# Routing of a PEER layer: second choice's one-hots in float16, scores used up in place, slots turned and first low parts made inside the first quarter of U

## The chip, the cores and the metric

The kernel runs on one core of a Trainium2 chip. The metric is the device time of one execution in microseconds (us); of several runs the median is given. A profiled execution has a time of its own, which is used for sums made from its rows. Engines: PE is TensorE, DVE is VectorE, ACT is ScalarE, POOL is GpSimd, SP is SyncE (it issues the weight transfers).

## The reference, cut to what matters

The model is a two-layer decoder step for 256 prompt tokens and 32 sample tokens, 288 tokens in all. Layer 0 is a gated MLP mixer, layer 1 dilated attention; each is followed by a PEER block, in which every token chooses 16 of 16384 experts in each of 8 heads:

```
q = (h @ w_q).reshape(T, PEER_HEADS, 2, D_HALF)
s = einsum('thpe,pke->thpk', q, sub_keys)                 # 2 x 128 scores a head
s1, i1 = top_k(s[:, :, 0], 16);  s2, i2 = top_k(s[:, :, 1], 16)
cand = s1[..., :, None] + s2[..., None, :]                # 256 candidates
top_s, top_c = top_k(cand, 16)
e1 = take_along_axis(i1, top_c // 16);  e2 = take_along_axis(i2, top_c % 16)
g = softmax(top_s)
a = einsum('td,thkd->thk', h, u_tab[e1 * 128 + e2])
coef = g * gelu(a)
out = einsum('thk,thkd->td', coef, v_tab[e1 * 128 + e2])
```

## The kernel before

Instead of gathering experts it multiplies all tokens by all of U (gelu of the result is C, laid out expert by token), scales C by a dense matrix of gates that is zero but at the chosen experts, and multiplies by all of V. The 128 tiles of 128 experts are taken in four quarters of 32 (`EQ`). `up` is a quarter of U, `down` one of V; the order is U0, U1, V0, U2, V1, U3, V2, V3 in each layer. U0 is done in plain float32 (`up_whole`: 32 tiles of 8 matmuls, PSUM banks 0 to 3 in turn). All other quarters split both operands into a high part (ScalarE, `upper_part`, for half a weight block) and a low part (VectorE, `lower_part`) and make three faster matmuls of each (`product`, L690, L691, L696).

Routing is done by VectorE during U0. `route(m, src, heads)` treats one tile of tokens: first the sample tile (m = 2, 2 heads' worth in 128 rows), then in a loop the two prompt tiles (m = 0, 1; 8 heads). `top16` finds the 16 largest scores with their places, two rounds of 8, and overwrites what it has found; for the prompt tiles a copy S of the scores S2 is made first (L1517), because a loop register picks the tile. The candidates are summed (L1495), `top16` again, then the two numbers of each choice are looked up: the place in the candidates is split into two (L1504, L1505), each is compared with 0..15 (L1508, 16 one-hots for 16 choices in 8 heads: 2048 elements), multiplied by the indices of the first selection (L1511) and reduced (L1514), all in float32. The results go to `eg`.

When the third tile is routed, VectorE raises `exp_in`; ScalarE takes the exponential (L1166); VectorE sums it, takes the reciprocal and scales (L1529 to L1534) and raises `slot_ready`. TensorE then transposes `eg` (`slot_transposes`, L644 and L648), VectorE copies the turned slots out of PSUM (L1552) and makes float16 copies (L1555 to L1559). From these come, during U1, the one-hots by token groups (`one_hot_group`, L1570 to L1579), whose product on TensorE is the gates (`gate_groups`, L664), applied by `apply_gates` (L1589). C's high and low parts are made at the start of a `down` (L1104, L1599).

Everything is ordered by hand: each engine has its own list, and semaphores count banks filled and emptied (`act_full`, `act_free`, `dve_full`, `dve_free`), blocks begun by TensorE (`blocks_begun`, on which SP reloads the ring of four 1 MB blocks), and high and low parts made (`hi_made`, `lo_made`). On TensorE `slot_transposes()` stands behind the whole of U0; on ScalarE the exponential and the first three high parts stand behind the activations of U0 (L1162); U1 on TensorE waits until the slots have been copied (`dve_free` at `D0["V"]`), for `h_lo` and for its first low part.

Of the kernel before, what the change touches and what calls it, by code (L numbers as in the profile page):

```python
# [32 lines left out]
ALU = mybir.AluOpType  # L33
# [64 lines left out]

GATE_LAG = 7
# [50 lines left out]
def build(nc, i, o):  # L150
    A0, D0 = starts(TO_ACT), starts(TO_DVE)
    with ExitStack() as ctx:
# [37 lines left out]
        iota_top, _ = place("iota_top", [P, TOP])  # L190
# [45 lines left out]
        S = view(big, EQ * T, HP, NK)  # L236
        cand = view(big, EQ * T + 2048, PH, TOP * TOP)
        eq = view(big, EQ * T + 4096, PH * TOP, TOP)
        tv = view(work, 0, HP, TOP)
        ti = work[:, 256:512].bitcast(U32).rearrange("p (a b) -> p a b", a=HP)  # L240
        tif = view(work, 512, PH, 2, TOP)
# [3 lines left out]
        posf = view(work, 1280, 2, PH * TOP)  # L245
# [197 lines left out]
        def _(pe):  # L443
# [177 lines left out]
            def peer(layer):  # L621
# [46 lines left out]
                def up_whole(q):  # L668
# [4 lines left out]
                    with pe.Fori(0, 2) as it:  # L673
                        for bl in range(8):
                            r = arrived(n0 + bl, it, 2)
                            for j in range(2 * bl, 2 * bl + 2):
                                pe.wait_ge(act_free, it * 16 + (k0 + j - 3))
                                for c in range(DC):
                                    at = ((j % 2) * DC + c) * P
                                    last = pe.matmul(ps[:, j % 4, 0:T], ring[:, r, at:at + P], hT[:, c, :],  # L680
                                                     start=(c == 0), stop=(c == DC - 1))
                                    if c == 0 and j % 2 == 0:
                                        last.then_inc(blocks_begun, 1)
                                last.then_inc(act_full, 1)
# [56 lines left out]
                slot_transposes()  # L741
# [245 lines left out]
        def _(act):  # L987
# [80 lines left out]
            def peer(layer):  # L1068
# [90 lines left out]
                with act.Fori(0, EQ // 8) as it:  # L1159
                    for j in range(8):  # L1160
                        act.wait_ge(act_full, it * 8 + (k0 + j + 1))
                        act.activation(C[:, 0, it * 8 + j, :], ps[:, j % 4, 0:T],  # L1162
                                       ACT.Gelu_apprx_tanh).then_inc(act_free, 1)

                act.wait_ge(exp_in, layer + 1)
                act.activation(gs, gs, ACT.Exp).then_inc(exp_out, 1)  # L1166
                for k in range(HI_LEAD):
                    upper_part(k)
# [104 lines left out]
        def _(dve):  # L1273
# [16 lines left out]

            def loop(n, per, body):

                n0 = count["n"]
                with dve.Fori(0, n) as it:
                    count["it"], count["per"] = it, per
                    body(it)
# [516 lines left out]
```

## Time and profile before

| | |
|---|---|
| median of 3 runs | 2414.11 us (2413.97 to 2414.7) |
| profiled execution | 2412.68 us, span 2410.9 us |
| PE busy | 2327.2 us, 97% of the span |
| DVE busy | 1590.8 us, 66% |
| ACT busy | 852.1 us, 35% |
| DMA | 348.93 MB, mean 145 GB/s |

The page gives busy times over the span, the chain of work that ended last, the costliest groups of instructions, and the DMA issues. Spans of matmuls overlap, so their mean duration is more than the time from one to the next. The profile can also be asked for the instructions in order of time, and for the busy time and the granted clock of TensorE in a stretch.

### The profile page before, as it was taken

Reading aid. Unit: us, or ns where it says so; the run is one execution under the profiler, and the core shown is the slowest. Engines: PE = TensorE matmul, PEld = TensorE weight load, DVE = VectorE, ACT = ScalarE, POOL = GpSimd, SP = SyncE. Lnnn points to the kernel's source line nnn. Section 1 sums busy time; section 2 is a strip of 40 time slices with the busy share of each in tenths; the row PEclk is TensorE's granted clock in tenths of the full one; section 3 lists DMA queues with packets and bytes.
Section 4 is the critical chain, followed back from the end, with each engine's and each line's share of the span. In section 5 each row is a group of like instructions: output and inputs, shape, how many; then the busy total and the mean of one; then the engine's idle time right before and its main releaser. Section 6 shows DMA issues by size and latency. Waiting matters only on the chain.

```text
span 2410.9 us, 47698 instructions
## 1 busy us (share of the span) xinstructions
PE 2327.2 (97%) x19577; PEld 2171.9 (90%) x19577; DVE 1590.8 (66%) x3496; ACT 852.1 (35%) x1137; POOL 55.8 (2%) x95
## 2 busy tenths in 40 slices
PE   7999999999999999999999999989999999999996
PEld 5889877999999999998987797789899999999996
DVE  5566599778755864686423359987787378548743
ACT  4534212342253244324323232133424432542432
POOL 1000000000000000002031000000000000000000
PEclk9999999999999999999999999999999999999998
DMA  5434343433454444446473243434344444444341
GB/s 205 162 105 158 123 140 110 142 133 127 140 171 157 140 141 173 141 141 215 162 245 129 87 139 123 139 122 141 123 140 150 164 141 139 163 169 141 124 155 72
DMA packets 51507, 348.93 MB, mean 145 GB/s; under 512 B 6369, under 2 KB 6385, under 8 KB 11665
## 3 DMA queue, kind: packets, MB, share of 16 engines
q1 hardware_dynamic: 44928, 324.16, 39.4%
q0 software_dynamic: 6448, 22.96, 3.0%
q8 instruction: 91, 1.49, 0.3%
q14 instruction: 40, 0.32, 0.0%
HBM read 342.83 MB, written 4.26 MB: 144 GB/s over the span
## 4 chain that ended last, share of the span: by engine, by line
PE 93%; ACT 3%; DVE 3%; issue 1%; DMA 0%; POOL 0%; DVEq 0%; ACTq 0%; POOLq 0%
PE ps L690 21%; PE ps L696 19%; PE ps L691 19%; PE ps L680 10%; PE ps L664 5%; PE ps L904 1%; PE ps L537 1%; ACT C_hi L1104 1%; PE ps L538 1%; PE ps L539 1%; PE ps L826 1%; PE ps L802 1%; PE ps L578 1%; PE ps L580 1%; PE ps L582 1%
## 5 line engine op out<-in xcount | busy, mean ns | idle before, releaser
L1544 DVE TENSOR_TENSOR w_lo<-ring,w_hi 128x1024 fp32r<-128x1024 f32 x448 | 544.0, 1221 | 268.0 <-ACT w_hi L1094 261.3
L1094 ACT ACTIVATE w_hi<-ring 128x1024 fp32r<-128x1024 f32 x448 | 473.3, 1058 | 638.0 <-PE ps L691 637.0
L690 PE MATMUL ps<-C_hi,w_hi 128*128 128x288 f32 x2048 | 627.3, 306 | 20.9 <-DVE C_lo L1599 20.6
L696 PE MATMUL ps<-C_hi,w_lo 128*128 128x288 f32 x2048 | 606.8, 296 | 0.0
L691 PE MATMUL ps<-C_lo,w_hi 128*128 128x288 f32 x2048 | 606.5, 296 | 0.0
L690 PE MATMUL ps<-h_hi,w_hi 128*128 128x288 f32 x1536 | 461.6, 301 | 4.1 <-DVE slots L1552 4.1
L691 PE MATMUL ps<-h_lo,w_hi 128*128 128x288 f32 x1536 | 454.9, 296 | 0.0
L696 PE MATMUL ps<-h_hi,w_lo 128*128 128x288 f32 x1536 | 453.3, 295 | 0.0
L690 PEld LDWEIGHTS ps<-C_hi,w_hi 128*128 128x128 f32 x2048 | 387.5, 189 | 26.5 <-DVE C_lo L1599 19.4
L691 PEld LDWEIGHTS ps<-C_lo,w_hi 128*128 128x128 f32 x2048 | 388.5, 190 | 0.0
L696 PEld LDWEIGHTS ps<-C_hi,w_lo 128*128 128x128 f32 x2048 | 387.9, 189 | 0.0
L690 PEld LDWEIGHTS ps<-h_hi,w_hi 128*128 128x128 f32 x1536 | 289.3, 188 | 4.3 <-issue 4.3
L696 PEld LDWEIGHTS ps<-h_hi,w_lo 128*128 128x128 f32 x1536 | 290.7, 189 | 0.0
L691 PEld LDWEIGHTS ps<-h_lo,w_hi 128*128 128x128 f32 x1536 | 290.0, 189 | 0.0
L680 PE MATMUL ps<-hT,ring 128*128 128x288 f32 x1024 | 248.8, 406 | 2.2 <-ACT mid L1155 2.2
L680 PEld LDWEIGHTS ps<-hT,ring 128*128 128x128 f32 x1024 | 194.4, 190 | 56.3 <-ACT mid L1155 2.7
L1116 ACT ACTIVATE big<-ps 128x288 f32 (+1 forms) x192 | 79.1, 412 | 351.5 <-PE ps L696 351.5
L1574 DVE TENSOR_TENSOR hots<-iota_twice,halves 128x1024 f16<-128x1024 f16 x288 | 196.7, 683 | 0.0
L664 PE MATMUL ps<-hots 128*128 128x32 f16 x4608 | 163.6, 177 | 0.0
L1606 DVE TENSOR_TENSOR xT<-xT,ps 128x288 f32<-128x288 f32 x64 | 29.1, 454 | 193.7 <-PE ps L696 193.7
L664 PEld LDWEIGHTS ps<-hots 128*128 128x128 f16 x4608 | 135.0, 97 | 21.1
L1579 DVE TENSOR_TENSOR hots<-hots,parts 128x256 f16<-128x256 f16 x576 | 139.7, 283 | 0.0
(252 smaller groups left out, 2508.9 us busy)
## 6 DMA issues: line engine op xcount, KB each, us to landing
ring<-in_U SPq DMA_DIRECT2D x128, 1024.0 KB, 4.9
ring<-in_V SPq DMA_DIRECT2D x128, 1024.0 KB, 4.9
ring<-in_peer_q SPq DMA_DIRECT2D x16, 1024.0 KB, 4.9
ring<-in_w_in_v SPq DMA_DIRECT2D x8, 1024.0 KB, 6.1
ring<-in_w_in_u SPq DMA_DIRECT2D x8, 1024.0 KB, 4.9
ring<-in_w_out SPq DMA_DIRECT2D x8, 1024.0 KB, 4.9
big<-in_cache POOLq DMA_DIRECT2D x16, 512.0 KB, 6.3
big<-in_cache POOLq DMA_DIRECT2D x48, 128.0 KB, 6.5
```

The source lines that it names most:

```text
L537: one = pe.matmul(out, ew_hi[:, h % HI_SLOTS, at], eh_hi[:, c, :], start=(c == 0), stop=False)
L664: g = pe.matmul(ps[:, 6 + j % 2, t * EQ:(t + 1) * EQ], hot1[:, j % RH, t // 2, :, t % 2], hot2[:, j % RH, c, t // 2, :, t % 2], start=(c = ...
L680: last = pe.matmul(ps[:, j % 4, 0:T], ring[:, r, at:at + P], hT[:, c, :], start=(c == 0), stop=(c == DC - 1))
L690: one = pe.matmul(out, w_hi[:, h % HI_SLOTS, at], hi, start=start, stop=False)
L691: two = pe.matmul(out, w_hi[:, h % HI_SLOTS, at], lo, start=False, stop=False)
L696: return pe.matmul(out, w_lo[:, h % (2 * R), at], hi, start=False, stop=stop)
L1094: act.activation(w_hi[:, k % HI_SLOTS, :], ring[:, bl % R, (k % 2) * HBLK:(k % 2 + 1) * HBLK], ACT.Copy).then_inc(hi_made, 1)
L1116: act.activation(C[:, q % 2, e, :], ps[:, h % 4, 0:T], ACT.Gelu_apprx_tanh).then_inc(act_free, 1)
L1544: dve.tensor_tensor(w_lo[:, n % (2 * R), :], ring[:, n // 2 % R, n % 2 * HBLK:(n % 2 + 1) * HBLK], w_hi[:, n % HI_SLOTS, :], ALU.subtract) ...
L1574: dve.tensor_tensor(hot1[:, s], iota_twice[:].unsqueeze(1).broadcast_to((P, pairs, NK, 2)), halves[:, 0, tok].rearrange("p (a t) -> p a t" ...
L1579: last = dve.tensor_tensor(hot2[:, s, c], here2, parts[:, c, tok].rearrange("p (a t) -> p a t", t=2).unsqueeze(2) .broadcast_to((P, pairs, ...
L1606: dve.tensor_tensor(xT[:, dc, :], xT[:, dc, :], ps[:, 4 + dc % 2, 0:T], ALU.add).then_inc(dve_free, 1)
```

## The change

The second lookup (the numbers of each choice) is done in float16: one-hots with the 16 places as the outermost dimension, elements in pairs, the sum over the places as four additions of halves in place of a reduction. The operands are copied as float16 beforehand (`tif` with each element twice, `posf` reordered). The prompt tiles are routed straight from S2, which is used up, without the copy and without the loop. The transposes of the slots stand ahead of tile 30 of U0 on TensorE (`SLOTS_EARLY = 2`); the exponential on ScalarE stands ahead of the activation of tile 28, and the first three high parts ahead of those of tiles 29, 30 and 31. The loops of `up_whole`, of its activations and of the routing are written out. `iota_top` goes; `iota_twice`, which the gates use already, takes its place.

```diff
--- before.py
+++ after.py
@@ -96,6 +96,8 @@
 HI_LEAD, LO_LEAD = 3, 2
 SPLIT = 7 * EQ
 
+SLOTS_EARLY = 2
+
 GATE_LAG = 7
 
 CCHUNKS = [(0, 1), (1, 3), (3, 6), (6, 10), (10, 14), (14, 19), (19, 25), (25, 32)]
@@ -187,7 +189,6 @@
         halves, _ = place("halves", [P, 2, T], F16)
         parts, _ = place("parts", [P, GATE_PARTS, T], F16)
         iota_twice, _ = place("iota_twice", [P, NK, 2], F16)
-        iota_top, _ = place("iota_top", [P, TOP])
         ident, _ = place("ident", [P, P])
         tmask, _ = place("tmask", [P, NS])
         ones, _ = place("ones", [P, P])
@@ -233,16 +234,16 @@
         qT = view(wide, 0, HP, T)
         S2 = view(mid, 0, 2, HP * NK)
         Ssam = view(mid, 2 * HP * NK, 2 * SH, NK)
-        S = view(big, EQ * T, HP, NK)
         cand = view(big, EQ * T + 2048, PH, TOP * TOP)
-        eq = view(big, EQ * T + 4096, PH * TOP, TOP)
+
+        eq = big[:, EQ * T + 4096:EQ * T + 5120].bitcast(F16)
         tv = view(work, 0, HP, TOP)
         ti = work[:, 256:512].bitcast(U32).rearrange("p (a b) -> p a b", a=HP)
-        tif = view(work, 512, PH, 2, TOP)
+        tif = work[:, 512:768].bitcast(F16).rearrange("p (s c) -> p s c", s=2)
         cs = view(work, 768, PH, TOP)
         pos = work[:, 896:1024].bitcast(U32)
         pos12 = work[:, 1024:1280].bitcast(U32).rearrange("p (a b) -> p a b", a=2)
-        posf = view(work, 1280, 2, PH * TOP)
+        posf = work[:, 1280:1408].bitcast(F16).rearrange("p (s n) -> p s n", s=2)
         gs = view(work, 1536, 2 * PH + SH, TOP)
         gsum = view(work, 1920, 2 * PH + SH)
         grec = view(work, 1944, 2 * PH + SH)
@@ -670,18 +671,18 @@
                     n0 = state["block"]
                     k0 = A0[f"U{layer}"] + q * EQ
                     pe.wait_ge(act_free, A0[f"U{layer}"])
-                    with pe.Fori(0, 2) as it:
-                        for bl in range(8):
-                            r = arrived(n0 + bl, it, 2)
-                            for j in range(2 * bl, 2 * bl + 2):
-                                pe.wait_ge(act_free, it * 16 + (k0 + j - 3))
-                                for c in range(DC):
-                                    at = ((j % 2) * DC + c) * P
-                                    last = pe.matmul(ps[:, j % 4, 0:T], ring[:, r, at:at + P], hT[:, c, :],
-                                                     start=(c == 0), stop=(c == DC - 1))
-                                    if c == 0 and j % 2 == 0:
-                                        last.then_inc(blocks_begun, 1)
-                                last.then_inc(act_full, 1)
+                    for j in range(EQ):
+                        r = arrived(n0 + j // 2)
+                        if j == EQ - SLOTS_EARLY:
+                            slot_transposes()
+                        pe.wait_ge(act_free, k0 + j - 3)
+                        for c in range(DC):
+                            at = ((j % 2) * DC + c) * P
+                            last = pe.matmul(ps[:, j % 4, 0:T], ring[:, r, at:at + P], hT[:, c, :],
+                                             start=(c == 0), stop=(c == DC - 1))
+                            if c == 0 and j % 2 == 0:
+                                last.then_inc(blocks_begun, 1)
+                        last.then_inc(act_full, 1)
                     state["block"] += EQ // 2
 
                 def product(out, h, tile, hi, lo, start, stop):
@@ -738,7 +739,6 @@
 
                 pe.wait_ge(h_ready, (1 + 2 * layer) * DC + DC)
                 up_whole(0)
-                slot_transposes()
                 pe.wait_ge(dve_free, D0[f"V{layer}"])
                 pe.wait_ge(h_lo_made, layer + 1)
                 up(1, 0)
@@ -1156,16 +1156,15 @@
                 act.wait_ge(h_ready, (1 + 2 * layer) * DC + DC)
                 act.activation(h_hi[:], hT[:], ACT.Copy).then_inc(h_hi_made, 1)
                 k0 = A0[f"U{layer}"]
-                with act.Fori(0, EQ // 8) as it:
-                    for j in range(8):
-                        act.wait_ge(act_full, it * 8 + (k0 + j + 1))
-                        act.activation(C[:, 0, it * 8 + j, :], ps[:, j % 4, 0:T],
-                                       ACT.Gelu_apprx_tanh).then_inc(act_free, 1)
-
-                act.wait_ge(exp_in, layer + 1)
-                act.activation(gs, gs, ACT.Exp).then_inc(exp_out, 1)
-                for k in range(HI_LEAD):
-                    upper_part(k)
+                for j in range(EQ):
+                    if j == EQ - SLOTS_EARLY - 2:
+                        act.wait_ge(exp_in, layer + 1)
+                        act.activation(gs, gs, ACT.Exp).then_inc(exp_out, 1)
+                    if j >= EQ - SLOTS_EARLY - 1 and j - (EQ - SLOTS_EARLY - 1) < HI_LEAD:
+
+                        upper_part(j - (EQ - SLOTS_EARLY - 1))
+                    act.wait_ge(act_full, k0 + j + 1)
+                    act.activation(C[:, 0, j, :], ps[:, j % 4, 0:T], ACT.Gelu_apprx_tanh).then_inc(act_free, 1)
                 up(0, 1)
                 down(1, split=0)
                 up(2, 2, split=1)
@@ -1287,15 +1286,6 @@
 
                 step(ins)
                 last_step()
-
-            def loop(n, per, body):
-
-                n0 = count["n"]
-                with dve.Fori(0, n) as it:
-                    count["it"], count["per"] = it, per
-                    body(it)
-                assert count["n"] == n0 + per, (count["n"] - n0, per)
-                count["it"], count["n"] = None, n0 + n * per
 
             def full(stage, k):
                 dve.wait_ge(dve_full, D0[stage] + k + 1)
@@ -1400,7 +1390,6 @@
 
             link(dve.tensor_reduce(tmask[:], ident[:].rearrange("p (a s) -> p s a", s=NS), AXX, ALU.add))
             dve.tensor_scalar(tmask[:], tmask[:], -1.0, 1.0e30, ALU.add, ALU.mult)
-            dve.tensor_copy(iota_top[:], iota[:, 0:TOP])
             dve.tensor_copy(iota_twice[:], iota.unsqueeze(2).broadcast_to((P, NK, 2)))
             dve.wait_ge(mix_loaded, 16 * 7)
             dve.tensor_tensor(wsp, wsp, maskp.unsqueeze(1).broadcast_to((P, AG, P)), ALU.mult)
@@ -1496,33 +1485,47 @@
                                            tv4[:, :, 0, :].unsqueeze(3).broadcast_to((P, heads, TOP, TOP)),
                                            tv4[:, :, 1, :].unsqueeze(2).broadcast_to((P, heads, TOP, TOP)), ALU.add))
                     link(top16(cs, pos.rearrange("p (a b) -> p a b", a=PH), cand, heads))
-                    dve.tensor_tensor(gs[:, bass.ds(m * PH, heads), :], cs[:, 0:heads, :],
+                    dve.tensor_tensor(gs[:, m * PH:m * PH + heads, :], cs[:, 0:heads, :],
                                       cs[:, 0:heads, 0:1].broadcast_to((P, heads, TOP)), ALU.subtract)
 
-                    dve.tensor_copy(tif.rearrange("p h s k -> p (h s k)")[:, 0:2 * n],
-                                    ti.rearrange("p a b -> p (a b)")[:, 0:2 * n])
                     dve.tensor_scalar(pos12[:, 0, 0:n], pos[:, 0:n], 4, None, ALU.logical_shift_right)
                     link(dve.tensor_scalar(pos12[:, 1, 0:n], pos[:, 0:n], 15, None, ALU.bitwise_and))
-                    link(dve.tensor_copy(posf[:, :, 0:n], pos12[:, :, 0:n]))
+                    half = TOP // 2
                     for s in range(2):
-                        link(dve.tensor_tensor(eq[:, 0:n, :], posf[:, s, 0:n].unsqueeze(2).broadcast_to((P, n, TOP)),
-                                               iota_top[:].unsqueeze(1).broadcast_to((P, n, TOP)), ALU.is_equal))
-                        eq4 = eq.rearrange("p (h k) j -> p h k j", h=PH)[:, 0:heads]
-                        link(dve.tensor_tensor(eq4, eq4,
-                                               tif[:, 0:heads, s, :].unsqueeze(2).broadcast_to((P, heads, TOP, TOP)),
-                                               ALU.mult))
-                        link(dve.tensor_reduce(eg[:, bass.ds(m, 1), s, 0:n], eq[:, 0:n, :], AXX, ALU.add))
-
-                def route_prompt(m):
-                    link(dve.tensor_copy(S.rearrange("p a b -> p (a b)").unsqueeze(1), S2[:, bass.ds(m, 1), :]))
-                    route(m, S, PH)
+                        dve.tensor_copy(
+                            tif[:, s, 0:2 * n].rearrange("p (j h t) -> p j h t", j=TOP, h=heads),
+                            ti.rearrange("p (h s) k -> p s k h", s=2)[:, s, :, 0:heads].unsqueeze(3).broadcast_to(
+                                (P, TOP, heads, 2)))
+                        last = dve.tensor_copy(
+                            posf[:, s, 0:n].rearrange("p (k h t) -> p k h t", k=half, h=heads),
+                            pos12[:, s, 0:n].rearrange("p (h k t) -> p k h t", h=heads, k=half))
+                    link(last)
+                    for s in range(2):
+                        link(dve.tensor_tensor(
+                            eq[:, 0:TOP * n].rearrange("p (j c t) -> p j c t", j=TOP, t=2),
+                            posf[:, s, 0:n].rearrange("p (c t) -> p c t", t=2).unsqueeze(1).broadcast_to((P, TOP, n // 2, 2)),
+                            iota_twice[:, 0:TOP, :].unsqueeze(2).broadcast_to((P, TOP, n // 2, 2)), ALU.is_equal))
+                        eq3 = eq[:, 0:TOP * n].rearrange("p (j k c) -> p j k c", j=TOP, k=half)
+                        link(dve.tensor_tensor(
+                            eq3, eq3,
+                            tif[:, s, 0:2 * n].rearrange("p (j c) -> p j c", j=TOP).unsqueeze(2).broadcast_to(
+                                (P, TOP, half, 2 * heads)), ALU.mult))
+
+                        for k in (8, 4, 2):
+                            link(dve.tensor_tensor(eq[:, 0:k * n], eq[:, 0:k * n], eq[:, k * n:2 * k * n], ALU.add))
+                        link(dve.tensor_tensor(
+                            eg[:, m, s, 0:n].rearrange("p (h k t) -> p k h t", h=heads, k=half),
+                            eq[:, 0:n].rearrange("p (k h t) -> p k h t", k=half, h=heads),
+                            eq[:, n:2 * n].rearrange("p (k h t) -> p k h t", k=half, h=heads), ALU.add))
 
                 dve.wait_ge(act_free, A0[f"U{layer}"])
                 route(2, Ssam, SH)
                 dve.wait_ge(h_hi_made, layer + 1)
                 dve.tensor_tensor(h_lo[:], hT[:], h_hi[:], ALU.subtract).then_inc(h_lo_made, 1)
-                loop(2, 1 + 3 + 1 + 1 + 3 + 1 + 2 + 6, route_prompt)
-                dve.wait_ge(dstep, count["n"])
+                for m in range(2):
+
+                    route(m, S2[:, m, :].rearrange("p (a k) -> p a k", a=HP), PH)
+                last_step()
 
                 dve.engine_nop().then_inc(exp_in, 1)
                 dve.wait_ge(exp_out, layer + 1)
```

## Rows read from the trace of the kernel before

**Rows 1.** Page: the chain that ended last, by engine.
```profile
PE 93%; ACT 3%; DVE 3%; issue 1%; DMA 0%; POOL 0%; DVEq 0%; ACTq 0%; POOLq 0%
```

**Rows 2.** By stretch: length, busy us (count) of PE, PEld, DVE, ACT, POOL; PEclk, DMA, GB/s.
```profile
278.00:402.50 124.50, 124.40 (x512) 97.20 (x512) 120.77 (x493) 19.55 (x36) 0.00 (x0) 1.00 0.39 135
402.50:410.20 7.70, 2.09 (x32) 1.61 (x31) 6.10 (x13) 7.21 (x8) 0.00 (x0) 0.74 0.00 0
410.20:530.00 119.80, 119.80 (x1331) 117.17 (x1332) 97.08 (x219) 43.22 (x62) 0.00 (x0) 0.99 0.41 141
```

**Rows 3.** Chain in order of time, layer 0: start, us, what.
```profile
278.10 124.44 PE ps L680 x512
...
403.09 1.28 ACT L1166
404.39 0.45 ACT work L1166
...
408.73 1.11 DVE slots L1552 x3
...
410.15 0.60 PE ps L690
```

**Rows 4.** The same chain, layer 1.
```profile
1450.93 124.44 PE ps L680 x512
...
1582.98 0.60 PE ps L690
```

**Rows 5.** Stretches behind the hole, columns as in rows 2.
```profile
410.10:413.20 3.10, 3.05 (x13) 3.05 (x14) 2.96 (x10) 0.00 (x0) 0.00 (x0) 0.53 0.36 71
1583.00:1587.30 4.30, 4.30 (x18) 4.30 (x19) 4.16 (x13) 2.34 (x2) 0.00 (x0) 0.51 0.57 198
```

**Rows 6.** VectorE in order of time: start, us, operation [idle before].
```profile
333.96 0.29 DVE L1499 TENSOR_TENSOR work<-work 128x128 f32 x1 [0.52 <-DVE work L1486]
...
349.80 1.23 DVE L1517 COPY big<-mid 128x2048 f32 x1 [0.56 <-DVE work L1514]
351.07 0.29 DVE L1472 MAX8 work<-big 128x8 f32<-128x128 f32 x1
...
388.11 0.29 DVE L1499 TENSOR_TENSOR work<-work 128x128 f32 x1 [0.29 <-DVE work L1486]
388.32 0.28 DVE L1502 CAST work<-work 128x256 f32<-128x256 uint32 x1
...
389.24 2.29 DVE L1508 TENSOR_TENSOR big<-work,iota_top 128x2048 f32<-128x2048 f32 x1
...
401.11 2.29 DVE L1514 TENSOR_REDUCE work<-big 128x2048 f32 x1
```

**Rows 7.** Groups of VectorE instructions by shape: busy us, mean ns.
```profile
L1574 DVE TENSOR_TENSOR hots<-iota_twice,halves 128x1024 f16<-128x1024 f16 x25 | 17.1, 685 | 0.0
L1579 DVE TENSOR_TENSOR hots<-hots,parts 128x256 f16<-128x256 f16 x50 | 12.2, 284 | 0.0
...
L1511 DVE TENSOR_TENSOR big<-big,work 128x2048 f32<-128x2048 f32 x4 | 9.2, 2292 | 0.1
...
L1511 DVE TENSOR_TENSOR big<-big,work 128x512 f32<-128x512 f32 x2 | 1.4, 691 | 0.1
```

**Rows 8.** TensorE in order of time at the transposes.
```profile
406.51 1.54 PE L644 MATMUL ps<-ident,work 128*128 128x128 f32 x6 [3.98 <-DVE work L1534]
...
1579.33 0.87 PE L644 MATMUL ps<-ident,work 128*128 128x128 f32 x6 [3.98 <-DVE work L1534]
...
1580.13 0.39 PE L648 MATMUL ps<-ident,work 32*32 32x32 f32 x24
```

**Rows 9.** ScalarE in order of time, end of the first quarter.
```profile
394.90 0.41 ACT L1162 ACTIVATE big<-ps 128x288 f32 x1 [3.47 <-PE ps L680]
```

**Rows 10.** Page: DMA issues, last number us to landing.
```profile
ring<-in_U SPq DMA_DIRECT2D x128, 1024.0 KB, 4.9
```

**Rows 11.** An unrolled stretch of TensorE, columns as in rows 2.
```profile
225.00:245.00 20.00, 19.98 (x150) 19.77 (x149) 16.10 (x24) 6.73 (x7) 0.00 (x0) 1.00 0.51 172
```

## The prediction, as put on record before the change was run

> **What bounds the kernel now.** I read the chain of waits by engine first [rows 1]: TensorE carries 93% of it, so a change pays only where it removes time in which TensorE stands still or runs slowly, or where it delays TensorE. Next the busy time by stretch round the changed place [rows 2]. In the first quarter of U (278 to 402.5) TensorE is busy 124.40 of 124.50 us, in the 7.7 us behind it 2.09 us, and in the quarter after that 119.80 of 119.80. VectorE is the one that is late: it is busy 120.77 us in the first stretch and its routing isn't done when TensorE is. The chain in order of time [rows 3] shows what fills the hole: TensorE's 512 matmuls end at 278.10 + 124.44 = 402.54, the exponential runs at 404.39, the turned slots are copied at 408.73, and the next quarter starts at 410.15. Layer 1 has the same chain [rows 4]: 1450.93 + 124.44 = 1575.37, next start 1582.98. Hole: 7.61 us in each layer, of which the slot transposes themselves are a part. Last, the clock behind the hole [rows 5]: granted 0.53 over 410.10 to 413.20 and 0.51 over 1583.00 to 1587.30, that is, nearly all at the lower level (1.2 GHz), after 4 us without any matmul and then only a few transposes.
>
> **The change, part by part.**
>
> *Two prompt tiles of routing on VectorE.* They use scores in place, so the copy goes: from its start 349.80 to the next instruction 351.07 is 1.27 us, twice, 2.5 us [rows 6]. The loop over them goes too: 0.56 us idle at its turn, and 0.52 us (first pass, and 0.29 in the second) ahead of L1499, the instruction addressed by a register, 1.4 us in all [rows 6].
>
> From L1499 to the end of the last reduction it is 388.11 to 403.40, 15.29 us a tile [rows 6]: 1.13 us of preparation, then six float32 passes over 2048 elements. The two float32 casts in it become four float16 ones; a 256-element cast takes 0.28 us, and it starts 0.08 us before the end of the independent instruction ahead of it [rows 6], so two of them are some 0.5 of the 1.13, 0.6 stay, and the new four take about 1.0 us, and 1.6 if the strided and repeated reads go at one element per cycle. Preparation 1.6 us, high end 2.2. The one-hots: float16 two-input instructions take 685 ns for 1024 elements and 284 ns for 256, so 0.15 us + 0.522 ns an element; float32 ones take 2292 ns for 2048 and 691 ns for 512, so 0.16 us + 1.042 ns [rows 7]. Per choice: compare and multiply, 2048 each, 2 x 1.22; sums in halves of 1024, 512 and 256, 0.69 + 0.42 + 0.28; the last of 128 into float32 taken at the float32 rate, 0.29. That is 4.12 us, and six waits on the result at 0.04 each (the copy at 349.80 takes 1.23 and its reader starts at 351.07), 4.36. Two choices: 8.7 us. Tail 10.3 against 15.29: 5.0 saved a tile, 10.0 for both. The sample tile (512 elements, six float32 passes of 0.69) goes from about 5.1 to 4.8 with the same two formulas: 0.2. Total 2.5 + 1.4 + 10.0 + 0.2 = 14.1 us, so the routing ends at 403.40 - 14.1 = 389.3.
>
> The compare and the multiply read operands that are repeated along an outer dimension and contiguous only in pairs (or in 16s). The row of L1574 has just that form of compare at 0.52 ns an element, and L1579 that of the multiply. The Trainium skill (VectorE: DVE Perf Modes, the section on how modes are chosen) says that a two-input instruction doubles its rate only if every tensor is 16-bit with step 1; this would leave the last sum, which writes float32, at the single rate. No row has such a mixed sum. By that page the sum is as above; at the double rate it would be 0.3 us shorter in all, hidden either way.
>
> *What the earlier end releases.* From the end of routing to the first transpose it is now 403.40 to 406.51 = 3.1 us, with a table load of 1.28 at 403.09 in front of the exponential [rows 3, 8, 9]. In the new order ScalarE comes to the exponential behind tile 27's activation (28 tiles, 278.10 + 28 x 3.889 = 387.0, plus 0.5), so the load runs 387.5 to 388.8, ahead of the scores. Exponential 389.4 to 389.8, the 1.67 us of reduction, reciprocal and scaling as before (404.84 to 406.51): slots ready at 391.5. TensorE arrives at the transposes ahead of tile 30, at 278.10 + 30 x 3.889 = 394.8. Slack 3.3 us: no wait.
>
> *The transposes.* They are not removed, only moved: 6 large and 24 small, 1579.33 to about 1580.52 = 1.2 us in layer 1 [rows 8]. In the new place they are between matmuls, so all 1.2 us are paid. U ends at 403.7.
>
> *ScalarE's moved work.* The activation of tile 28 has the second table load before it: exponential out 389.8, load to 391.1, tile full at 390.9; 0.2 us late, and its bank is wanted only by the next quarter's first tile. The three high parts (1.06 each) go in front of the activations of tiles 29, 30, 31, where ScalarE now idles 3.47 of each 3.88 us [rows 9]. Their blocks are in the ring: SP's reload waits for blocks that TensorE has begun, in the same order as before; the block for the third part is issued when tile 28 begins (387.0) and a block lands in 4.9 us [rows 10]. SP's queue itself isn't changed, and POOL's isn't passed.
>
> *VectorE behind the slots.* First low part 392.9 to 394.1, second 396.3 to 397.5 (it waits for the second high part), three copies 1.2, halves and parts 1.5, two groups of one-hots 2.6: done about 403. TensorE's next quarter wants the slots copied, one low part and a free bank at 403.7: all there. VectorE then waits for tile 31's activation (404.2) before its third low part, which TensorE wants two rounds of some 3.3 us later. So nothing is late next, and the hole closes entirely. If the float16 casts or sums cost up to 3.3 us more than worked out, still nothing; beyond it each microsecond is a stall of one in each layer.
>
> *Unrolled code.* TensorE's, ScalarE's and VectorE's loops are now written out. TensorE's unrolled projection of 225 to 245 runs 150 matmuls in 20.00 us, 0.133 each with nothing lost [rows 11], faster issue than the 0.243 needed here. And the loop's 512 matmuls are at 0.243 throughout, so its turn costs nothing now. Taken: 0, bounds -0.3 and +1.5 us a layer. The Trainium skill (Runtime: NRT & Kernel Launch, Instruction fetch mechanics) says that a taken branch can force a fetch stall and straight code is prefetched; by it the unrolling might also give TensorE something at the turn, but the constant 0.243 shows nothing to give, and on VectorE the 0.56 is in the sum already.
>
> *Clock.* TensorE never idles before the quarter, so I expect the 0.51 to 0.53 rows to become 1.00. 13 matmuls in 3.10 us would take 13 x 0.133 = 1.73: 1.4 saved; 18 in 4.30 would take 2.4: 1.9 saved [rows 5, 11].
>
> **The sum.** Per layer 7.61 - 1.2 = 6.4; twice 12.8; clock 1.4 + 1.9 = 3.3; together 16.1 us. The profiled execution took 2412.68 us (span 2410.9): 2396.6. The median of the runs is 2414.11, 1.43 above it, so in terms of the median **2398.0 us**.
>
> **Rivals.**
> *A, the slots come late by a little.* The four casts, the strided last sum or the extra dependent waits cost more than 3.3 us above my 14.1. For it: none of these forms has a row, and there are six dependent steps a choice where there were three. Against it: even all sums at one element per cycle add 4 x 0.95 = 3.8 and the casts 1.2, 5.0 together, 1.7 over the slack. 2 x 1.7 = 3.4 back, and perhaps no loss of clock for so short a stop: 2401.4.
> *B, the float16 passes run at the single rate.* Then a choice costs 2 x 2.29 + 1.22 + 0.69 + 0.43 + 0.29 + 0.24 = 7.45 us, two tiles 29.8 for the one-hots instead of 17.4; with the slower casts (1.2 more) routing ends at 389.3 + 12.4 + 1.2 = 402.9 and the slots are ready at 405.1 or later. TensorE stands at tile 30 from 394.8, 10.3 us instead of 6.4 net, because the two tiles that used to cover the wait now lie behind it; the clock drops there as it did before. 3.9 lost a layer: 2414.1 + 7.8 = 2421.9. It decides against the change once the slots are ready after 394.8 + 6.4 = 401.2. Against: L1574 and L1579 [rows 7].
> *C, given back downstream.* The next quarter would be bound by VectorE and eat the gain. For it: VectorE is busy 97.08 of 119.80 us there [rows 2], and C_lo later makes TensorE wait. Against: 23 us idle, TensorE busy all 119.80, and VectorE's own start there moves forward by about 10 us, more than TensorE's. If half of the gain went: 2406.
> *D, nothing gained*, something unseen on the path in place of the hole (fetching code, a reload): 2414.
>
> **How the numbers follow.** Forecast 0.83 (2395 to 2400.5), A 0.06, B 0.03, C 0.04, D 0.04. Changes under 0.2%, 4.8 us, can't be told from none here. Forecast, A and C are faster; D is no change or slightly slower; B slower: 0.93, 0.03, 0.04. The range reaches from 2394.5 (unrolling gains, routing's end lets VectorE run ahead and shortens a later C_lo wait) to 2403, which takes in A.
>
> **What would show it.** The row of the quarter's 512 matmuls grows from 124.4 to some 125.7 from first start to the next quarter's first, with the transposes inside it and no wait on the slots. The last routing instruction ends near 389.3 (wrong if after 392.6). L1508's successor, the float16 compare of 2048, takes 1.2 us, not 2.3. The 0.51 and 0.53 clock rows are 1.00. The next quarter and the C_lo waits keep their length. I am wrong if TensorE shows a wait at the transposes, if any 3 us of it are at half clock behind U's first quarter, or if the C_lo waits grow by microseconds.

## The result and the profile after

| | before | after |
|---|---|---|
| median, first comparison | 2414.4 us (2413.97 to 2416.77) | 2394.74 us (2394.41 to 2396.8) |
| ratio, 95% interval | | 0.9922 [0.991, 0.9935] |
| the changed kernel again (second comparison) | 2413.94 us | 2397.02 us, 0.993 [0.9913, 0.9946] |
| and a third time | 2413.91 us | 2396.42 us, 0.9925 [0.9912, 0.9939] |
| profiled execution, span | 2410.9 us | 2392.6 us |
| PE / DVE / ACT busy | 2327.2 / 1590.8 / 852.1 us | 2322.0 / 1565.7 / 843.9 us |

The change is faster by 17 to 20 us, 0.7 to 0.8%. The forecast was 2398.0 in a range of 2394.5 to 2403.0.

The chain of the changed kernel in order of time, layer 0 and then layer 1 (start, us, what), answers to [rows 3, 4]:

```profile
277.08 0.73 issue
277.82 116.64 PE ps L681 x480
394.45 0.66 PE ps L645 x6
395.11 0.32 PE ps L649 x24
395.43 7.96 PE ps L681 x32
...
406.16 0.41 PE ps L665 x16
...
1440.64 0.73 issue
1441.38 116.64 PE ps L681 x480
1558.02 0.65 PE ps L645 x6
...
1558.99 7.96 PE ps L681 x32
1569.74 0.41 PE ps L665 x16
```

No other engine stands in it: TensorE goes from tile 29 into the transposes (L645, L649), on to the last two tiles and into the next quarter. To compare kernels I take one length from this view, "the stage": from the end of the last score matmul to the start of the first gate group (the first of the groups of 16 matmuls that make the gates, L665 here, L664 before). In both kernels 21 matmuls of the second quarter lie ahead of that group. Before, the rows are these:

```profile
267.22 9.82 PE ps L633 x96
277.06 0.61 ACT mid L1155
277.67 0.43 issue
...
414.49 0.41 PE ps L664 x16
...
1440.02 9.82 PE ps L633 x96
...
1587.92 0.41 PE ps L664 x16
```

Before: 277.04 to 414.49 = 137.45 us and 1449.84 to 1587.92 = 138.08. After: 277.08 to 406.16 = 129.08 and 1440.64 to 1569.74 = 129.10. Gain 8.37 and 8.98, together 17.35 us of the 18.3 us of span. It splits into four parts, by subtraction of the rows:

| us | forecast | layer 0 | layer 1 |
|---|---|---|---|
| hole of 7.61, less transposes of 0.98 | 6.4 | 6.63 | 6.64 |
| first 21 matmuls at full clock (4.34 and 4.94 before, 2.77 and 2.79 now) | 1.4, 1.9 | 1.57 | 2.15 |
| start of U's first quarter (1.06 and 1.09 before, 0.74 now) | 0 | 0.32 | 0.35 |
| its 512 matmuls (124.44 before, 124.60 now) | 0 | -0.16 | -0.16 |

By stretch, with the columns of rows 2 (it answers to [rows 2, 5]):

```profile
403.00:523.50 120.50, 120.50 (x1346) 117.69 (x1344) 95.39 (x212) 44.55 (x64) 0.00 (x0) 1.00 0.42 140
410.10:413.20 3.10, 3.10 (x37) 3.03 (x37) 2.41 (x6) 1.39 (x2) 0.00 (x0) 1.00 0.38 87
```

The granted clock is 1.00 through the whole next quarter, and in the stretch in which it was 0.53. The matmuls of U's first quarter and the transposes among them take 116.64 + 0.98 + 7.96 = 125.58 us in place of 124.44, where the prediction's sign said some 125.7. VectorE in order of time, the second prompt tile's lookup and what follows it (it answers to [rows 6]):

```profile
378.93 0.29 DVE L1488 TENSOR_TENSOR work<-work 128x128 f32<-128x128 f32 x1
...
379.88 0.29 DVE L1495 CAST work<-work 128x256 f16<-128x256 uint32 x1
...
380.33 1.22 DVE L1504 TENSOR_TENSOR big<-work,iota_twice 128x2048 f16<-128x2048 f16 x1
...
382.85 1.48 DVE L1515 TENSOR_TENSOR big<-big 128x1024 f16<-128x1024 f16 x3
...
384.69 1.23 DVE L1504 TENSOR_TENSOR big<-work,iota_twice 128x2048 f16<-128x2048 f16 x1
...
388.72 0.29 DVE L1516 TENSOR_TENSOR work<-big 128x128 f32<-128x128 f16 x1
...
390.65 0.59 DVE L1537 TENSOR_TENSOR work<-work 128x128 f32<-128x128 f32 x3
```

One choice takes 384.69 - 380.33 = 4.36 us, the figure of the forecast. The preparation takes 1.40 (1.6 forecast), the tail 10.08 (10.3). The routing ends at 389.01 (389.3), the slots are scaled at 391.24 (391.5), and TensorE takes them at 394.45.

### The profile page after: what moved, and what is told of

Same layout as the page of the kernel before. It is cut to its first block, busy times and chain, and to the rows that moved or that the text cites. A ratio compares the mean times of both kernels' runs of the same rounds, so it can differ in the third digit from the quotient of the medians.

```text
span 2392.6 us, 47473 instructions
## 1 busy us (share of the span) xinstructions
PE 2322.0 (97%) x19577; PEld 2167.2 (91%) x19577; DVE 1565.7 (65%) x3539; ACT 843.9 (35%) x1131; POOL 55.7 (2%) x95
## 4 chain that ended last, share of the span: by engine, by line
PE 94%; ACT 3%; DVE 2%; issue 1%; DMA 0%; POOL 0%; DVEq 0%; ACTq 0%; POOLq 0%
PE ps L691 21%; PE ps L697 20%; PE ps L692 19%; PE ps L681 10%; PE ps L665 5%; PE ps L904 1%; ACT C_hi L1104 1%; PE ps L538 1%; PE ps L539 1%; PE ps L540 1%; PE ps L579 1%; PE ps L826 1%; PE ps L802 1%; PE ps L583 1%; PE ps L581 1%; PE ps L634 1%
## 5 line engine op out<-in xcount | busy, mean ns | idle before, releaser
L691 PE MATMUL ps<-C_hi,w_hi 128*128 128x288 f32 x2048 | 626.5, 306 | 20.8 <-DVE C_lo L1602 20.3
L665 PE MATMUL ps<-hots 128*128 128x32 f16 x4608 | 163.6, 177 | 0.0
L665 PEld LDWEIGHTS ps<-hots 128*128 128x128 f16 x4608 | 134.9, 97 | 21.3
```

The source lines that it names most:

```text
L665: g = pe.matmul(ps[:, 6 + j % 2, t * EQ:(t + 1) * EQ], hot1[:, j % RH, t // 2, :, t % 2], hot2[:, j % RH, c, t // 2, :, t % 2], start=(c = ...
L691: one = pe.matmul(out, w_hi[:, h % HI_SLOTS, at], hi, start=start, stop=False)
```

## The experiments

Unless said otherwise each edit is made to the changed kernel. "Stage" is the length defined above; "rest" is the span less both stages, work that no edit here touches (but the last, and but for one small copy at the start, that of `iota_top`). "On the same chip" means a comparison made together; the kernel before had 2413.94 in the one with the second run of the changed kernel and 2413.91 in the one with the third.

| kernel | median us | ratio to before, interval | stage, layer 0 / 1 | rest |
|---|---|---|---|---|
| before | 2414.4 | | 137.45 / 138.08 | 2135.4 |
| after | 2394.74 | 0.9922 [0.991, 0.9935] | 129.08 / 129.10 | 2134.4 |
| after, second | 2397.02 | 0.993 [0.9913, 0.9946] | 129.10 / 129.09 | 2137.1 |
| after, third | 2396.42 | 0.9925 [0.9912, 0.9939] | 129.10 / 129.09 | 2136.5 |
| order only | 2423.41 | 1.0034 [1.0022, 1.0045] | 142.48 / 142.71 | 2135.3 |
| routing only | 2414.78 | 1.0 [0.9991, 1.001] | 137.45 / 137.77 | 2138.5 |
| float32 lookup | 2416.22 | 1.0004 [0.9994, 1.0014] | 138.71 / 138.62 | 2137.5 |
| one pass of delay | 2396.68 | 0.9929 [0.9912, 0.9945] | 129.10 / 129.10 | 2136.1 |
| two passes of delay | 2401.14 | 0.9943 [0.9926, 0.996] | 130.81 / 130.81 | 2137.7 |
| one tile earlier | 2398.02 | 0.9936 [0.9923, 0.995] | 130.05 / 130.04 | 2135.6 |
| two tiles earlier | 2410.49 | 0.9985 [0.9975, 0.9995] | 135.51 / 136.84 | 2134.7 |
| loops only | 2412.94 | 0.9996 [0.9987, 1.0006] | 137.29 / 137.22 | 2137.3 |
| parts of C ahead | 2392.95 | 0.9911 [0.9898, 0.9925] | 129.09 / 129.10 | 2133.0 |

My theory: TensorE gained because the slots are ready before it needs them, which takes both halves of the change, the shorter routing and the new order. Rivals: one half is enough; or the gain comes from the written-out code.

**Order only** (the kernel before with the new order; lookup, copy and routing loop as before):

```diff
+                    for j in range(EQ):
+                        if j == EQ - SLOTS_EARLY:
+                            slot_transposes()
...
+                    if j == EQ - SLOTS_EARLY - 2:
+                        act.wait_ge(exp_in, layer + 1)
+                        act.activation(gs, gs, ACT.Exp).then_inc(exp_out, 1)
...
-                slot_transposes()
```

> Kernel before with the new order alone: transposes ahead of tile 30, exponential ahead of tile 28, high parts among the last activations, loops of U's first quarter written out; lookup in float32, copy and routing loop kept. My theory: the order pays only if the routing ends in time. It ends at 403.4 as before, so the slots are ready at about 405.6 while TensorE stands at tile 30 from 394.5: a stall of 11 us in place of 6.5, tiles 30 and 31 behind it, partly at the lower clock. 4.5 to 6.5 us lost per layer: 2423 to 2428 us against 2414.4. Rival (the order is what pays, VectorE's time matters little): 2400 to 2410.

Measured 2423.41 us, slower than before. Its chain, layer 0:

```profile
278.18 116.64 PE ps L682 x480
394.81 11.44 issue
406.25 1.51 PE ps L646 x6
...
408.24 8.89 PE ps L682 x32
```

TensorE stands 11.44 us ahead of the transposes (10.94 in layer 1), which then take 408.24 - 406.25 = 1.99 instead of 0.98, and the two tiles 8.89 instead of 7.96. What used to cover the wait now stands behind it. The new order alone costs 5.0 and 4.6 us a layer.

**Routing only** (the old order with the new routing):

```diff
-                        if j == EQ - SLOTS_EARLY:
-                            slot_transposes()
...
+                slot_transposes()
```

> Kernel after with the old order: transposes, exponential and first high parts behind the whole first quarter, TensorE's and ScalarE's loops kept; float16 lookup, scores in place, routing written out. My theory: the routing ends at 389 but nothing waits for it there; ScalarE comes to the exponential only at 403.1 and the hole stays 7.6 us: 2413 to 2414.5 us, the same as before within 1.5 us. Rival (14 us less of VectorE's work pay by themselves): 2404 or less.

Measured 2414.78, ratio 1.0 [0.9991, 1.001]: the same. Its chain:

```profile
278.42 124.44 PE ps L681 x512
...
404.70 0.45 ACT work L1167
```

The exponential starts 404.70 - 278.42 = 126.28 us after U does; before it was 404.39 - 278.10 = 126.29 [rows 3]. Some 14 us less of VectorE's work move nothing, since ScalarE comes there only behind its last activation and a table load. VectorE's last sum of the lookup starts at 388.98, and it then stands idle until the exponential is there:

```profile
388.98 0.29 DVE L1518 TENSOR_TENSOR work<-big 128x128 f32<-128x128 f16 x1
405.18 0.45 DVE L1534 TENSOR_REDUCE work<-work 128x18 f32<-128x288 f32 x1 [15.91 <-ACT work L1167]
```

So neither half pays alone, one even loses, and together they give 17.

The new order moves three things at once: the exponential, the transposes and the first high parts. No run moves one of them alone, so what share each has isn't shown. Of the hole before, TensorE's stop ahead of the transposes was 3.98 us [rows 8]. A second stop of 1.63 us in layer 0 and 2.45 in layer 1 came behind them, while VectorE copied the slots (1.11 us). In layer 1 the transposes were over at 1580.52 [rows 8], but VectorE was at two low parts until 1581.55, which held the copy up by 1 us:

```profile
1579.28 2.27 DVE w_lo L1544 x2
```
```profile
410.15 0.60 PE L690 MATMUL ps<-h_hi,w_hi 128*128 128x288 f32 x1 [1.63 <-DVE slots L1552]
1582.98 0.60 PE L690 MATMUL ps<-h_hi,w_hi 128*128 128x288 f32 x1 [2.45 <-DVE slots L1552]
```

With the shorter routing, moving the exponential alone could have removed the first stop, as VectorE's idle 15.91 us show. That is argued from rows, and no run tests it.

**Float32 lookup** (copy and loop gone, new order, but compare, multiply and reduce as before):

```diff
-                        for k in (8, 4, 2):
-                            link(dve.tensor_tensor(eq[:, 0:k * n], eq[:, 0:k * n], eq[:, k * n:2 * k * n], ALU.add))
...
+                        link(dve.tensor_reduce(eg[:, m:m + 1, s, 0:n], eq[:, 0:n, :], AXX, ALU.add))
```

> Kernel after with the float32 lookup of the kernel before (compare, multiply, reduce over 2048 elements); scores in place, loops written out and the new order kept. My theory: the routing ends about 4 us earlier than before, at 399.5, the slots are ready at 401.6, TensorE stands 7 us at tile 30 where 3 us of slack were: the stall eats the 6.5 us and the clock loss returns: 2412 to 2417 us. Rival (leaving out the copy and the loop is enough): under 2405.

Measured 2416.22, ratio 1.0004 [0.9994, 1.0014]. Its chain and the stretch behind the stop:

```profile
395.48 7.07 issue
```
```profile
402.55:407.60 5.05, 5.05 (x37) 3.80 (x38) 4.02 (x7) 2.19 (x3) 0.00 (x0) 0.50 0.19 31
```

Stop 7.07 as forecast; stage 9.61 longer than after, 2.54 more than the stop. Nearly all of that is the clock (0.50 granted behind the stop). Without float16 the rest of the change is worth nothing.

**Delays: how large is the slack?** One or two dependent float32 passes ahead of the exponential:

```diff
+                for _ in range(2):
+                    link(dve.tensor_tensor(cand, cand, cand, ALU.max))
                 dve.engine_nop().then_inc(exp_in, 1)
```

> Kernel after with two more dependent float32 passes over 2048 elements (each cand = max(cand, cand), 2.33 us) on VectorE ahead of the exponential. My theory: slack is 3.15 us (slots ready at 391.3, TensorE at the transposes at 394.45), so 4.66 us of delay stall TensorE 1.5 us in each layer and the clock stays: plus 3.0 us, 2397 to 2398.5 against 2394.7. Rival 1 (slack is larger, something else sets the transposes): no change. Rival 2 (any stop there drops the clock): plus 6 to 10 us.

> Kernel after with one more float32 pass over 2048 elements (2.33 us) ahead of the exponential. My theory: slack is 3.2 us (routing end plus 2.25 = 391.3 against 394.45), so the delay is hidden: time as after within 1 us, 2394 to 2396.5. Rival (in the run with two passes only 3.4 of the 6.4 us lost lay in the stages; the other 3 come with any delay): 2397 or more.

Two passes: 2401.14. Chain, layer 0:

```profile
280.23 116.64 PE ps L681 x480
396.87 1.54 issue
398.41 0.85 PE ps L645 x6
```

The stop is 1.54 (1.5 forecast) and each stage 1.71 longer, 3.4 us together. The median is another matter. It rose by 6.4 over the first runs of the changed kernel, which is above my range (2397 to 2398.5) and within that of rival 2, a fall of the clock. The clock did not fall. This is the stretch behind the stop in layer 0, and layer 1 has 1.00 there too:

```profile
398.41:407.60 9.19, 9.19 (x64) 7.30 (x65) 7.59 (x17) 3.57 (x6) 0.00 (x0) 1.00 0.34 115
```

3.3 us lie in the rest, 2137.7 against 2134.4; 2.4 of them are already there when the first stage begins (279.50 against 277.08). The changed kernel itself had 2137.1 in its second profile, so I don't count them as the delay's; what they come from stays open. One pass: 2396.68 against 2397.02 of the changed kernel on the same chip, and the stages are the same to 0.02 us. So the delay is hidden, though the median lies just over a range that counted from the first runs. The other 3 us of the rival don't come. VectorE's last instruction ahead of the transposes, and their start on TensorE:

```profile
393.47 0.59 DVE L1539 TENSOR_TENSOR work<-work 128x128 f32<-128x128 f32 x3
```
```profile
394.96 0.66 PE ps L645 x6
```

The slots are ready at 394.06, 0.90 us before TensorE comes: slack 0.90 + 2.33 = 3.2 us, 3.3 forecast.

**Transposes one and two tiles earlier:**

```diff
-SLOTS_EARLY = 2
+SLOTS_EARLY = 3
```

The second run has 4 there. The exponential and the first high parts move along with the transposes.

> Kernel after with the transposes one tile earlier, ahead of tile 29: TensorE is there at 390.56, the slots are ready at 391.26, a stall of 0.7 us in each layer, no fall of the clock: 1.4 us over the changed kernel; the stage 128.95 to 129.1 us. Rival (the clock falls after any stop): 3 to 5 us over it.

> Kernel after with the transposes two tiles earlier, ahead of tile 28, exponential and high parts likewise. TensorE comes there at 386.7, the slots are ready at 391.3: it stands 4.6 us in each layer. Stall alone: plus 9.2, 2404 us. If the clock falls, as it did for the stops of 7.1 and 11.4 us but not for that of 1.5 us, 2 to 2.5 us more a layer: 2408 to 2409. I take the second, since the hole of the kernel before was 4.0 us up to the transposes.

One tile: stop 0.76 us, stage 0.95 longer in each layer, 2398.02 against 2396.42 on the same chip. Two tiles: 2410.49 against 2397.02, 13.5 us lost. That is above the 2408 to 2409 of the expectation, which counted from the first runs; the loss itself is the one forecast for a falling clock (9.2 for the stop and 4 to 5 for the clock). In the stages it is 14.2. Chains of both layers of the second kernel, and the stretches behind the stop:

```profile
387.27 4.64 issue
391.91 0.85 PE ps L645 x6
...
1556.02 4.64 issue
1560.66 1.51 PE ps L645 x6
```
```profile
391.91:395.20 3.29, 3.29 (x34) 2.53 (x35) 2.30 (x2) 2.19 (x3) 0.00 (x0) 0.61 0.03 7
1560.66:1567.40 6.74, 6.74 (x41) 5.09 (x42) 5.61 (x11) 2.19 (x3) 0.00 (x0) 0.54 0.35 103
```

The same stop of 4.64 us cost 6.41 us in layer 0 (1.77 over the stop) and 7.74 in layer 1 (3.10). The stops of 0.76 and 1.54 us cost only themselves and 0.2. So in these runs a stop of 4.6 us or more was paid again in clock, with 1.8 to 3.1 us a layer, and the amount differed between layers of one kernel; why it did isn't shown.

**Loops only** (the kernel before, TensorE's and ScalarE's loops in U's first quarter written out, order as before):

```diff
-                    with pe.Fori(0, 2) as it:
-                        for bl in range(8):
...
+                    for j in range(EQ):
+                        r = arrived(n0 + j // 2)
+                        pe.wait_ge(act_free, k0 + j - 3)
```

> Kernel before with only the loops of TensorE and ScalarE in U's first quarter written out. My theory: nothing, 2413.5 to 2415.5 us, matmuls at 0.243 us as in the loop. Rival (written out code lets the engines fetch more smoothly and gives the 1.6 us gained outside the stage): 2412 to 2413. Rival (fetching costs): over 2416.

Measured 2412.94, ratio 0.9996 [0.9987, 1.0006]: no difference that can be told. The median lies in the range of the first rival, but the kernel before had 2413.94 in this comparison, and the rest, in which that rival put its gain, is 2137.3 against 2135.4, not shorter. The chain shows a small difference:

```profile
276.97 1.23 PE ps L633 x18
278.20 0.73 issue
278.93 124.41 PE ps L678 x512
```

0.73 us from the last score matmul to the first of U, as in the changed kernel; with the loop it is 1.06. The first matmul waits for ScalarE's last copy of the scores, and 0.43 passed behind it, up to the start at 278.10 [rows 3]; written out, the matmul comes 0.09 behind that copy (278.24 + 0.60 to 278.93). I read the difference as the setting up of TensorE's loop; ScalarE's was written out in the same run. The 512 matmuls take 124.41 against 124.44. The stage of layer 1 is 0.86 shorter, of which this start is 0.35; the rest lies in the hole and behind it, where the kernels with a stop do not repeat as closely as the changed one (routing only has 137.77 there).

**The changed kernel again.**

> The changed kernel once more, beside the three below. U's first quarter up to its 565th matmul should again take 128.3 us in each layer, and the time be 2394 to 2397 us. What differs in the rest of the span from the first profile (start, attention, tail) is what executions of one program differ by: I expect up to 2 us there. Rival: the rest repeats to 0.3 us, then the 1.6 us gained outside the changed stage belong to the change.

> The changed kernel a third time, as the comparison for the two below on one chip: 2394.5 to 2397.5 us, its two changed stages 128.3 us up to the 565th matmul.

The 128.3 us of the expectations run from the first matmul of U, 0.74 us behind the start of my stage: 129.08 less 0.74. The changed kernel's stages repeat to 0.02 us, the rest doesn't: 2134.4, 2137.1, 2136.5, a little more than the 2 us that I expected. So what the first comparison shows beyond 17.35 us isn't the change's: in the other two the medians differ by 16.9 and 17.5.

**A version that is faster than both.** With the hole gone the next thing that TensorE waits for in each layer is C_lo (the low parts of C) at the start of V's first quarter. ScalarE makes the high parts behind its last activation of the quarter before, though it and VectorE are idle there:

```diff
+AHEAD = 3
...
+                            if h == EQ - 1:
+                                upper_part(k0 + h)
+                                gates_applied(0)
+                                upper_C(0, CCHUNKS[:AHEAD])
...
+                        if nth == 1:
+                            dve.wait_ge(gate_free, (layer * NQ + 1) * NGG + CREDIT)
+                            lower_C(0, list(range(AHEAD)))
                         dve.wait_ge(act_free, A0[f"U{layer}"] + (gates + 1) * EQ)
```

> Kernel after, and in each layer the first three pieces of the high and low parts of C for V's first quarter are made before the activation of the second U quarter's last tile, in ScalarE's and VectorE's waiting time there (the last gate is applied at 520.8, ScalarE is free at 521.8, VectorE at 523.3, TensorE begins V at 523.7). Theory: VectorE starts its low parts at 523.3 in place of 524.6, so the C_lo waits of V's first quarter get 1.3 us shorter in each layer, and perhaps the 3.4 us at the lower clock behind them go (1.7 us a layer): 2.6 to 6 us under the changed kernel. Rival (ScalarE's chain of high parts sets the waits later in that quarter, not its start): under 1 us.

Measured 2392.95 us (2390.2 to 2395.34), 0.9911 [0.9898, 0.9925] of before; the changed kernel on the same chip 2396.42 (2394.53 to 2397.66). 3.5 us faster by the medians, with ranges that overlap, so the medians alone don't settle it. The 22 us from the end of U's second quarter in layer 1, first the changed kernel, then this one:

```profile
1687.50:1709.50 22.00, 17.32 (x122) 15.91 (x121) 15.80 (x16) 12.85 (x13) 0.00 (x0) 0.92 0.29 96
```
```profile
1687.30:1709.30 22.00, 17.82 (x148) 16.20 (x147) 17.33 (x19) 13.00 (x12) 0.00 (x0) 1.00 0.32 101
```

And the waits of TensorE at the start of V in layer 0, the changed kernel's and this one's:

```profile
PE ps L691 <- DVE C_lo L1602: 5.0, 4, 2.0
```
```profile
PE ps L692 <- DVE C_lo L1614: 3.5, 4, 1.8
```

1.5 us less wait in layer 0 (1.3 forecast), but only 0.4 less in layer 1 (4.2 against 4.6), where the clock is 1.00 in place of 0.92. What settles it is a length again: from the end of the stage to the first matmul of U's third quarter, that is, the rest of U's second quarter and all of V's first. In this kernel the stages end at 408.93 and 1570.70, and these are the first matmuls of U's third quarter:

```profile
653.06 0.29 PE L692 MATMUL ps<-h_hi,w_hi 128*128 128x288 f32 x1
1814.24 0.29 PE L692 MATMUL ps<-h_hi,w_hi 128*128 128x288 f32 x1
```

The lengths are 244.13 and 243.54 us. The three profiles of the changed kernel have 245.92, 245.33 and 245.99 in layer 0 and 245.96, 245.33 and 245.32 in layer 1. So 1.2 to 2.4 us are gained in each layer, 3.0 to 4.2 in both, in the range forecast.

## Why the prediction was right

*The bound.* The hole of 7.61 us a layer lay on the path, as read, and it closed entirely.

*VectorE's sum.* Routing end forecast 389.3, measured 389.01, from the loops' and copies' rows and two straight lines through float16 and float32 rows. 4.36 us a choice was exact. The pairwise repeated operands keep the float16 rate (2048 elements 1.22 us). The last sum, float16 in and float32 out, takes 0.29 us for 128 elements, as the float32 line gives; by the float16 line (0.15 us + 0.522 ns an element) it would be about 0.22. The Trainium skill's condition for the doubled rate (VectorE: DVE Perf Modes, the section on how modes are chosen) is that every tensor is 16-bit with step 1, and this row agrees with it. The casts with repeated reads were cheaper than my high end: 0.29 us for 256 elements, where the float32 line would give 0.43. That the end was right to 0.3 us did not decide the time: any end up to 3.2 us later gives the same.

*The slack.* 3.3 forecast, 3.2 shown by the delays. Rival A was right in its price (a stop of one microsecond for each beyond the slack) and didn't come about. Rival B's mechanism is real: the float32 lookup put the slots ready 7.07 us after TensorE came, and the gain was gone. Its break-even, slots 6.4 us late, fits too: at 7.07 the stages are 1.26 and 0.54 us longer than before. But the float16 passes ran at the double rate. Rivals C and D are out. The next quarter stayed TensorE's (120.50 of 120.50 us busy), TensorE's waits for C_lo are 20.3 us in the whole span against 20.6 before, and the length from the first gate group to U's third quarter is 245.3 to 246.0 us in the profiles of the changed kernel against 245.73 and 245.00 before: at most 1.0 us a layer is given back.

*The sum.* 16.1 forecast for what measured 17.35 in the stages. The 1.25 between them: 0.67 at the start of U's first quarter, which I had costed at nothing (bound -0.3 a layer; 0.32 and 0.35 measured), 0.47 because the transposes take 0.98 and not 1.2, 0.42 of clock, less 0.32 for the 512 matmuls. The row of the transposes that I used stands behind a stop of 3.98 us, with a granted clock of 0.92; between matmuls they are shorter. The first comparison's 19.66 goes beyond 17.35 by what lies in the rest, where executions of this kernel differ by 2.7 us; my 2398.0 was nearest to the second and third sets (2397.02 and 2396.42). The sum fell short in three terms, all small, and no large error was hidden by another.

*Unrolled code.* The reading that the turn of the loop costs TensorE nothing was right (124.41 against 124.44), that writing it out saves nothing was not: 0.32 and 0.35 us go ahead of the first matmul, just past the bound of 0.3. That the loops alone gave 2412.94 against 2413.94, within the interval, fits it but doesn't prove it; the rows do.

## What to carry to other kernels

Moving a consumer earlier and making its producer shorter can be worthless or harmful apart and pay together: compare when the producer ends with when the consumer arrives, and move it no farther than the slack (here 3.2 us; in the stages one tile of 3.9 us farther cost 1.9 us, two tiles 14.2). Before shortening an engine's work look whether its consumer is queued behind something else; here 14 us less of VectorE's gave nothing until exponential, transposes and high parts were moved ahead. Where a stage repeats to 0.02 us, judge an edit by the stage and not by the whole time, which here moved by 2.7 us between profiles of one kernel.

## What the runs showed of the hardware that I had not expected

A stop of 4.64 us of TensorE cost 1.77 us beyond itself in one layer and 3.10 in the other, nearly all of it clock, with the same code before and behind it. In layer 0 the transposes right behind the stop still ran at full speed (0.85 us) and the clock was low only after that; in layer 1 they were slow already (1.51). Stops of 0.76 and 1.54 us cost 0.2 us beyond themselves: the six transposes behind the stop of 1.54 take 0.85 us in place of 0.66, at a granted clock of 1.00. With TensorE's loop, U's first matmul came 0.3 us later than with the code written out, though the loop itself ran at full rate.
